# A layer kernel's expert lookup: one-hots from digit codes, fourteen kept tiles, earlier first picks, and a new split of the weighing

## The reference, cut to what matters

```
q = (h @ w_q).reshape(B, S, 8, 2, 128)
s1, s2 = q[..., 0, :] . sub_keys_1, q[..., 1, :] . sub_keys_2     # 128 scores each
v1, i1 = top_k(s1, 16);  v2, i2 = top_k(s2, 16)
cand = v1[:, None] + v2[None, :]                                  # 256 pairs
top, pos = top_k(cand, 16);  eidx = i1 * 128 + i2 at pos          # one of 16384 experts
gate = softmax(top)
act = gelu(einsum('td,tkd->tk', h, expert_u[eidx]))               # 8 * 16 = 128 experts a token
out = einsum('tk,tkd->td', gate * act, expert_v[eidx])            # d = 2048
```

## Time and profile before

| | |
|---|---|
| median of three runs | 1931.37 us |
| the profiled execution, its own time | 1930.16 us |
| its span | 1928.4 us |
| busy PE / DVE / ACT / POOL | 1833.6 / 1317.2 / 389.7 / 750.5 us |
| mean granted clock of PE | 0.985 |

### The profile page before, as it was taken

One profiled execution on the slowest core, in us unless ns is written; L12 is line 12 of the kernel. 1 busy time (PEld: TensorE's weight loads), 2 busy tenths in 40 slices (PEclk: granted clock), 3 DMA queues, 4 the chain that ended last, 5 costly groups with the idle time before them and its releaser, 6 DMA issues.

```text
span 1928.4 us, 28418 instructions
## 1 busy us (share of the span) xinstructions
PE 1833.6 (95%) x10929; PEld 1415.7 (73%) x10929; DVE 1317.2 (68%) x2611; ACT 389.7 (20%) x842; POOL 750.5 (39%) x789
## 2 busy tenths in 40 slices
PE   3899999999999999999999999888989999999997
PEld 3787787777875458888888888778876666656664
DVE  5855666666662333598999975799986666666666
ACT  3022222222222020011111111588740000000001
POOL 2002212222111000365444443338895786744552
PEclk8789999999999999999999999999999999999999
DMA  9956656765581954989999999876449999999997
GB/s 396 420 200 263 228 197 248 292 249 210 213 345 54 402 204 157 370 323 410 405 407 402 402 410 409 327 230 205 144 154 408 409 409 408 409 408 409 409 406 284
DMA packets 124382, 609.09 MB, mean 316 GB/s; under 512 B 15584, under 2 KB 15712, under 8 KB 101216
## 3 DMA queue, kind: packets, MB, share of 16 engines
q1 hardware_dynamic: 66496, 330.33, 44.0%
q0 software_dynamic: 57344, 274.76, 37.3%
q10 hardware_dynamic: 416, 2.25, 0.3%
HBM read 603.09 MB, written 4.19 MB: 315 GB/s over the span
## 4 chain that ended last, share of the span: by engine, by line
PE 81%; DVE 8%; DMA 7%; issue 2%; POOL 2%; ACT 1%; DVEq 0%; SPq 0%; ACTq 0%
PE ps L1413 22%; PE ps L1330 20%; PE ps L996 14%; PE ps L1045 6%; PE ps L1235 6%; DMA arena<-in_v_dense 3%; PE ps L1084 3%; DVE arena L1474 2%; DVE ps L1802 2%; PE ps L1385 2%; DVE arena L1794 2%; DMA arena<-in_ada 2%; POOL arena L615 2%; DMA arena<-in_w_in 1%; PE ps L1356 1%
## 5 line engine op out<-in xcount | busy, mean ns | idle before, releaser
L1413 PE MATMUL ps<-arena 128*128 128x368 f32 x1536 | 477.4, 473 | 7.7 <-DMA arena<-in_v_dense 7.0
L1413 PEld LDWEIGHTS ps<-arena 128*128 128x128 f32 x1536 | 300.9, 196 | 182.8 <-DMA arena<-in_v_dense 10.9
L1863 DVE SCALAR_TENSOR_TENSOR arena<-arena 128x944 f32<-128x944 f32 x254 | 305.2, 1201 | 173.7 <-DMA arena<-in_v_rows,arena 172.3
L599 POOL DMA_INDIRECT arena<-in_u_rows,arena x256 | 257.6, 1006 | 346.6 <-DVE arena L1794 287.2
L1330 PE MATMUL ps<-arena 128*128 128x256 f32 x1792 | 386.9, 379 | 0.0
L1330 PEld LDWEIGHTS ps<-arena 128*128 128x128 f32 x1792 | 340.5, 190 | 46.1
L599 POOL DMA_INDIRECT arena<-in_v_rows,arena x256 | 295.7, 1155 | 182.3 <-DVE arena L1863 149.4
L996 PE MATMUL ps<-arena 128*128 128x256 f32 x1440 | 349.4, 386 | 2.6 <-DMA arena<-in_w_in 2.6
L1794 DVE SCALAR_TENSOR_TENSOR arena<-arena,ps 128x1152 f32<-128x1152 f32 x208 | 277.8, 1349 | 52.8 <-DMA arena<-in_u_rows,arena 52.2
L996 PEld LDWEIGHTS ps<-arena 128*128 128x128 f32 x1440 | 261.8, 190 | 40.6 <-DMA arena<-in_w_in 4.2
L1453 DVE SCALAR_TENSOR_TENSOR arena<-arena 128x2048 f32<-128x2048 f32 x60 | 143.5, 2392 | 24.8 <-DMA arena<-in_ada 24.7
(11 more groups left out here) (251 smaller groups left out, 1746.0 us busy)
## 6 DMA issues: line engine op xcount, KB each, us to landing
arena<-in_ada SPq DMA_DIRECT2D x96, 1024.0 KB, 7.4
arena<-in_v_dense SPq DMA_DIRECT2D x128, 552.0 KB, 8.7
arena<-in_u_dense SPq DMA_DIRECT2D x128, 448.0 KB, 7.1
arena<-in_w_in SPq DMA_DIRECT2D x45, 1024.0 KB, 7.3
arena<-in_w_tail SPq DMA_DIRECT2D x32, 1024.0 KB, 9.1
arena<-in_w_in SPq DMA_DIRECT2D x12, 512.0 KB, 16.6
arena<-in_u_rows,arena POOLq DMA_INDIRECT x256, 10.1
arena<-in_v_rows,arena POOLq DMA_INDIRECT x256, 11.7
```

The source lines that it names most:

```text
L599: nc.gpsimd.indirect_dma_start(out=row, out_offset=None, in_=table[:, :], in_offset=bass.IndirectOffsetOnAxis(ap=i32(idx[:, b, k:k + 1]), ...
L1413: last = mm(sums(b)[:, g, :], dense[:, b, j // 2, :, j % 2], w[:, g * VG:(g + 1) * VG], start=(j == 0), stop=(j == NKEYS - 1))
L1863: stt(total[b], row, w, total[b], ALU.mult, ALU.add).then_inc(v_sum, 1)
```

## The change

It has five parts.

**Codes.** VectorE splits each chosen first key into two digits (`make_digits`) and writes the digits and their squares in bf16; ScalarE's queue stores them to a DRAM tensor `codes` (in the dense u stage, at tile 112). For each group of four tokens a small DMA on SP's queue (`code_tile`, 4 rows of 4x128 bf16) fetches its codes into one of two tiles. One bf16 matmul with prepared weights `code_w` (from 14 more GpSimd instructions ahead of the gathers) leaves a number from which a single Relu with a bias for each partition (`make_bias`) makes the four one-hots. `hot_out` counts one a group instead of two.

**Kept tiles.** Fourteen instead of ten: tiles 18, 24, ... 96. Six of them are loaded during the output projection (`EARLY_KEPT`); `qT` is cut to a quarter for their room.

**First picks.** The transposes of the second keys and `spread_keys(0)` stand before tile 125's products; ScalarE copies and makes the first one-hots before it evacuates tile 126. The exponentials move to tile 112. `turn_weights(0)` stands one group later.

**Dots.** 202 instead of 198 before the picks; in the first half groups 0, 3, ... 27 have none.

**Weighing.** In groups 33, 36, ... 63 VectorE makes all four weights. GpSimd makes five groups' for four u gathers instead of four.

```
@@ loads
+            def keep_tile(n):
+                product_tile(KEPT[KEPT_ORDER.index(n)])
+
             for n in range(6, 22):
...
                 sp.dma_start(ring[:, m % WSLOTS, :], w_tail[n]).then_inc(land[m % WSLOTS], 16)
+                if n in EARLY_KEPT:
+                    keep_tile(EARLY_KEPT[n])
...
+            def code_tile(q):
+
+                b, t = divmod(4 * q, P)
+                if q == 0:
+                    sp.wait_ge(code_zero, 2)
+                    sp.wait_ge(digits_saved, 16 * TB)
+                if q >= 4 and q % 2 == 0:
+                    sp.wait_ge(spread, q - 2)
+                rows = code[q // 2 % 2][4 * (q % 2):4 * (q % 2) + 4, :]
+                sp.dma_start(rows.rearrange("r (t k) -> r t k", t=4), codes[b, t:t + 4].rearrange("t r k -> r t k")).then_inc(code_land[q % 4], 16)
+
+            for q in range(T // 4):
+                code_tile(q)
             for j in range(NKEYS, 2 * NKEYS):
@@ GpSimd
-            for n in range(TB * KTOP):
+            weighed = 0
+            for n in range(NROWS):
...
-                if n >= WEIGH_AT:
-                    weigh(n - WEIGH_AT)
+                while n >= WEIGH_AT and weighed < min(5 * (n - WEIGH_AT + 1) // 4, P // 4):
+                    weigh(weighed)
+                    weighed += 1
@@ ScalarE
+            def one_hot(q):
+
+                act.wait_ge(spread, q + 1)
+                if q >= 2:
+                    act.wait_ge(turned, q - 1)
+                nc.scalar.activation(hot[q % 2].rearrange("p a b -> p (a b)"), bank(0), ACT.Relu, bias=one_minus).then_inc(hot_out, 1)
+
...
                 if j == NKEYS - D // P:
                     act.wait_ge(picked, 8)
+                    act.wait_ge(digits_made, TB)
+                    for b in range(TB):
+                        act.dma_start(codes[b], digits[b]).then_inc(digits_saved, 16)
...
-                nc.scalar.activation(h, bank(0), ACT.Abs, bias=minus_p).then_inc(hot_out, 1)
-                act.wait_ge(hot_out, 2 * q + 1)
-                nc.scalar.activation(h, h, ACT.Relu, bias=ones[:, 0:1], scale=-1.0).then_inc(hot_out, 1)
@@ TensorE
+            def spread_keys(q):
+
+                if q % 2 == 0:
+                    for n in range(2):
+                        pe.wait_ge(code_land[(q + n) % 4], 16 * (q // 4 + 1))
+                if q:
+                    pe.wait_ge(hot_out, q)
+                mm(bank(0), code_w[q % 2], code[q // 2 % 2], start=True, stop=True).then_inc(spread, 1)
+
             for j in range(NKEYS):
+                if j == NKEYS - 3:
...
+                    spread_keys(0)
...
-                if q == P // 4 + 2:
+                if q == P // 4 + 3:
                     turn_weights(0)
@@ VectorE
-                if q >= P // 4 or q % 16 not in (5, 10, 15):
+                if q not in NO_DOT:
                     dots(ndot[0], ndot[0] + 1)
@@ numbers
-LATE = TB * KTOP - 58
-KEPT = tuple(24 + 6 * n for n in range(10))
+LATE = 202
+NO_DOT = (0, 3, 6, 9, 12, 15, 18, 21, 24, 27)
+KEPT = tuple(18 + 6 * n for n in range(14))
+EARLY_KEPT = {8: 2, 10: 3, 12: 4, 14: 5, 16: 12, 18: 13}
...
-WEIGH_AT = TB * KTOP - 24
-POOL_TOKENS = ((2, 3), (3,))
+WEIGH_AT = 232
...
+def pool_tokens(q):
+    return (2, 3) if q < P // 4 else (3,) if q % 3 else ()
```

More of the change, by code:

```diff
@@ L101, in build_layer @@
 def build_layer(nc, x, cols, ada, w_in, w_tail, lora_up, keys,
-                u_dense, u_rows, v_dense, v_rows, out):
+                u_dense, u_rows, v_dense, v_rows, out, codes):
     with ExitStack() as ctx:
@@ L229, in build_layer @@
         top[0] = max(top[0], ring_at + SL)
+        route_at = take(0)
+        repl = new(D // 4)
+        cand = new(2, TOPK * TOPK)
         v16, i16 = new(2 * 2, TOPK), new(2 * 2, TOPK)
         iu = new(2 * 2, TOPK)
-        repl_at = take(0)
-        repl = new(D // 4)
-        cand = new(2, TOPK * TOPK)
-        hot = [view(repl_at, 4, P), view(repl_at + 4 * P, 4, P)]
+        topv, pos, hi_u, lo_u, hi_f, lo_f = (new(2, TOPK) for _ in range(6))
+        hot = [view(route_at + n * 4 * P, 4, P) for n in range(2)]
+        code = [colp[:, 0:2 * P].bitcast(BF16), view(route_at + 8 * P, 2 * P).bitcast(BF16)]
+        assert route_at + 10 * P <= take(0)
         eq = new(2 * TOPK, TOPK)
-        topv, pos, hi_u, lo_u, hi_f, lo_f = (new(2, TOPK) for _ in range(6))
-        iota, minus_p = new(P), new(1)
+        iota, one_minus = new(P), new(1)
         iota16 = iota[:, 0:TOPK]
@@ L242, in build_layer @@
         idx2T = new(T)
-        ident_h = new(P // 2).bitcast(BF16)
-        idx1_h = [new(KTOP // 2).bitcast(BF16) for _ in range(TB)]
         actv, wv = new(TB, KTOP), new(TB, KTOP)
+        digit_at = [take(0) - TB * KTOP, take(2 * KTOP)]
+        digits = [view(a, 2 * KTOP).bitcast(BF16).rearrange("p (t k) -> p t k", t=4) for a in digit_at]
+        code_w = [ones[:, n * KTOP // 2:(n + 1) * KTOP // 2].bitcast(BF16) for n in range(2)]
         assert take(0) <= ring_at + 3 * SL
@@ L604, in _, with number, settled @@
             nc.gpsimd.iota(iota, [[1, P]], base=0, channel_multiplier=0, allow_small_or_imprecise_dtypes=True).then_inc(numbers, 1)
-            nc.gpsimd.iota(minus_p, [[1, 1]], base=0, channel_multiplier=-1, allow_small_or_imprecise_dtypes=True).then_inc(numbers, 1)
+            made = [1]
+            def number(ins):
+                made[0] += 1
+                ins.then_inc(numbers, 1)
+            def settled():
+                pool.wait_ge(numbers, made[0])
+            high, low, coded, part = (view(a, P) for a in (digit_at[0], digit_at[0] + P, digit_at[1], digit_at[1] + P))
+            number(nc.gpsimd.iota(high, [[2, 8], [0, 16]], base=0, channel_multiplier=0, allow_small_or_imprecise_dtypes=True))
+            number(nc.gpsimd.iota(low, [[0, 8], [2, 16]], base=0, channel_multiplier=0, allow_small_or_imprecise_dtypes=True))
+            nc.gpsimd.memset(colp[:, 0:2 * P], 0.0).then_inc(code_zero, 1)
+            for n in range(2):
+                settled()
+                number(nc.gpsimd.affine_select(out=coded, in_=high, compare_op=ALU.is_equal, fill=0.0, base=-4 * n, pattern=[[0, P]], channel_multiplier=1))
+                number(nc.gpsimd.affine_select(out=part, in_=low, compare_op=ALU.is_equal, fill=0.0, base=-4 * n - 2, pattern=[[0, P]], channel_multiplier=1))
+                settled()
+                number(nc.gpsimd.tensor_tensor(coded, coded, part, ALU.add))
+                for r in (1, 3):
+                    settled()
+                    number(nc.gpsimd.affine_select(out=coded, in_=coded, compare_op=ALU.not_equal, fill=-1.0, base=-4 * n - r, pattern=[[0, P]], channel_multiplier=1))
+                settled()
+                number(nc.gpsimd.tensor_copy(code_w[n], coded))
+            assert made[0] == NUMBERS
             pool.wait_ge(w_used, WOUT + 16 + 5)
             def weigh(q):
-                if q % (P // 4) == 0:
+                if not pool_tokens(q):
+                    return
+                if q in (0, P // 4, P // 4 + 1):
                     pool.wait_ge(wT_out, 4 * q // P + 1)
@@ L630, in _ @@
                 if n == 0:
-                    for q in range(TB * KTOP - WEIGH_AT, P // 4):
+                    for q in range(weighed, P // 4):
                         weigh(q)
@@ L1804, in _ @@
             dve.wait_ge(w_used, WOUT + 16 + 2)
[L1805 to L1806 removed]
+            dve.wait_ge(numbers, 1)
             route(0, 0)
@@ L2024 @@
     out = nc.dram_tensor("out_0", (T, D), F32, kind="ExternalOutput").ap()
-    build_layer(nc, *aps, out)
+    codes = nc.dram_tensor("first_key_codes", (TB, P, 4, KTOP), BF16).ap()
+    build_layer(nc, *aps, out, codes)
     r = run(nc, [ins], core_ids=[0])
```

139 lines of the change are left out of this document (85 added, 54 removed).

## The result

The changed kernel took 1939.74 us (median of 6 runs, 1935.48 to 1941.88), the kernel before 1931.3 on the same chip: a ratio of 1.0035, with a 95% interval of 1.0023 to 1.0046. By this ratio it is slower by 6.7 us (4.4 to 8.9; the two medians alone are 8.4 apart), and its median lies outside the range of 1924.5 to 1934.5. Its profiled execution took 1935.48 us, the shortest of the six; the one of before had 1930.16.

The account below looks back on a forecast made before the run. Dense stages were full, so only the 206 us of picking and weighing between them, paced by VectorE, could gain. 1.6 - 5.1 - 0.3 + 3.0 - 1.5 = -2.3 us gave 1929.1 us, range 1924.5 to 1934.5.

Parts of the forecast that it names:

- the split: Weighing behind the last pick: VectorE makes all four weights in every third group, six groups from 6.15 to 5.8 us; -1.5.
- Start of the picks: End of dense u stage: TensorE waits 3.6 us for codes before the first spread, first pick at 1233.7; +1.6 us.
- the upper end: Start of the picks: codes landing after 8.1 us, 2.7, plus 1.7 for a half-speed clock; 4.4 us.
- Rival A: Codes are there in time, no TensorE stop at tile 125, first pick 2.0 earlier; -5.9, 1925.5; chance 0.17.
- Four dots fewer: Picking: 54 instead of 58 dots behind the first pick, 1.28 us of VectorE each; -5.1 us.
- the cheaper one-hots: Picking: a 723 ns ScalarE pass less per group, but ScalarE was idle where VectorE was full; 0.
- rival C: First half of picking: each pair of code tiles comes late, 1.6 x 15 = 24 us slower, 1953; chance 0.08.
- the 2.6 of a short load: Evidence cited against late code tiles in the first half: a 256 KB load alone took 2.6 us.
- The later transpose of the weights: Early picking: `turn_weights(0)` a group later removes a wait of TensorE that reached VectorE; -0.3 us.
- GpSimd's five groups for four gathers: Last four dots: gathers behind more weighing come late, VectorE waiting 1.5 us twice; +3.0 us, bounds 0 and +3.4.
- The v stage: Dense v sums after the weighing: as long as before, 486 to 487 us, moving as a whole.
- D: Early tiles delay the output projection, or the digits delay the dots; up to +6, 1935; chance 0.05.

Follow-up runs that it names:

- e1: Changed kernel with GpSimd weighing one group behind each gather again, not five for four; 1933.34 us, ratio 1.0004 to the kernel before.
- e4: Changed kernel with GpSimd again making one of the four weights in every group of the second half; 1940.94 us, ratio 1.0041 to the kernel before.
- e2: Changed kernel with SP sending the first four code tiles ahead of u tile 122, not behind the last u tile; 1933.74 us, ratio 1.0000.
- e7: Changed kernel with one group of GpSimd's weights behind each gather and the first spread ahead of tile 127, not 125; 1928.24 us, ratio 0.9976.
- e6: Kernel before with one edit alone: five groups of GpSimd's weights behind four gathers; 1936.24 us, ratio 1.0015.
- e9: Changed kernel, codes ahead of u tile 122, GpSimd weighing two groups behind gather 232, one behind every later gather; 1931.40 us, ratio 0.9991.
- e12: Changed kernel unchanged, run again for a second trace; 1937.80 us, ratio 1.0027 to the kernel before.
- e5: Changed kernel, codes ahead of u tile 122, one group of GpSimd's weights per gather, plus TensorE matmuls nobody reads; 1925.59 us, ratio 0.9964.
- e10: e5 with GpSimd again making one weight in every group of the second token block; 1926.22 us, ratio 0.9969 to the kernel before.

## Why the prediction was wrong, step by step

Three steps failed. The wait of TensorE for the codes was mis-sized, and the slow clock behind it stood at nothing in the sum (1.6 forecast, 4.8 measured). GpSimd's lead was priced as late rows alone, and what it does to VectorE's own weights in every group was missed (3.0 forecast, 5.2 measured: 2.7 for the late rows, 2.5 for the collision). And the split was put at -1.5 where it is worth 0.

- **Start of the picks, +1.6: the mechanism was right, the size was not; 4.8.** The codes did queue behind the last u tile. They landed after 7.9 us, not the median 7.0, and left SP a little later against the start of the stage: 1.3 together. The clock fell behind the stall, 1.8, which I had seen in the trace and put only into the upper end, where it belonged in the sum: a dense engine that stands for 4 or 5 us was a surer case than the one-column matmuls from which I took the price. All four traces with the stall have the fall (3.4 us long in two, 6.8 in e1 and e4). The upper end of 4.4 was nearly the value. Run e2 gives the whole term back. Rival A would have needed e2's order, and got 0.9 there, not its 2.0.
- **Four dots fewer, -5.1: right, -4.7.** VectorE had 4.95 us less to do in this half (69.12 and 64.17 busy) and stood 0.2 longer. Nothing came back in the dense stage, whose last dot ended at 1227.6, as forecast. That the cheaper one-hots cost and gain nothing fits this sum; no run has them alone. The codes are in time from group 1 on (no wait of TensorE for them between 1235 and 1298): rival C falls in the changed kernel, but not by much. A pair has 4.4 to 6.3 us from its issue to its spread there, and in e2 and e7 one pair took 5.8 and 5.5 us and held TensorE up for 0.9 and 1.0; the 2.6 of a short load was no price for it. The later transpose of the weights: picks 32 to 36 took 10.0 instead of 10.4, the -0.3, also without a run of its own.
- **GpSimd's five groups for four gathers, +3.0: the wait was right, a second loss was missed.** Picks 60 to 63 took 2.3 us longer, in the second trace 3.4: the late rows, forecast as 3.0, though as one wait of 1.9 to 2.1 and a rest and not as two of 1.5. Missing is the line of VectorE's weights: once GpSimd is as far ahead as its three slots let it be, TensorE's products start its pair, and this puts it onto VectorE's two instructions in every group from the eighth to the twenty-fourth: 0.81 us for 0.60. Picks 48 to 60 lose 1.3, and picks 36 to 48 1.2 (35.6 for 34.4). I had reasoned about GpSimd as a supplier that could only be late, and never asked what it does to VectorE by being early. The trace of the kernel before had it: 0.78 in its groups 24 to 27, and its last dots 2.98 us apart instead of 2.87. e1 takes the lead out of the change, e6 puts it alone into the kernel before, and e9 has the collision without the late rows.
- **The split, -1.5: wrong, 0.** GpSimd has two instructions less in six groups, but they were not what TensorE waited for any more: with slots for three groups, GpSimd can begin a weight only when the products three groups back are done, and the gather then stands between two of them (1414.04, 1415.14 and 1416.19 in the changed kernel). That the gather is what holds the round at 6.2 us is argued from these times; no run moves it. VectorE's instructions for the fourth weight fall beside GpSimd's, which took 0.87 to 0.94 each instead of 0.82. Without a clock fall there are 42.3 us in the changed kernel (e12) and 42.0 before; with TensorE busy 42.6 with and without the split (e5, e10).
- **The v stage**: 487.3 and 488.0 against 486.5 and 487.0. I had it unchanged; other traces of both families lie between 486.5 and 488.0, so no cause is sought.

By the first traces the terms are 4.8 - 4.7 + 4.4 + 0.4 (between the last pick and the last dot) + 1.1 + 0.9 = 6.9 us, where the runs gave 6.7. That they agree so well is partly luck. The two profiled executions themselves are only 5.3 us apart, since the stages ahead of the dense products were 1.8 us shorter in that of the changed kernel (the first dense product comes at 837.7 to 843.2 us in the fourteen traces, in no order that the edits explain). And by the second traces the same terms are 4.3 - 4.9 + 5.5 + 0.0 - 1.9 + 1.0 = 4.0, where the ratio of e12 gives 5.2 (3.1 to 7.4); the weighing behind the last dot is 1.1 in one pair and -1.9 in the other, by where the clock fell. The forecast had -2.3. Of the 9.2 us between it and the first traces 3.2 are the start, 2.6 the split with the clock fall, 2.1 the second half (4.4 and 0.4 where 3.0 less 0.3 stood), 0.9 the v stage and 0.4 the dots. The chances failed too: all rivals but C and D were faster ones, though each price of the slower side (the clock, GpSimd's limit) lay in the rows.

## What to carry to other kernels

A helper engine that runs ahead is not free: when its slots are full, the consumer's pace triggers it at one fixed moment of each round, and if that moment falls on the critical engine's own work of the same kind, every round can pay (here 5%, 0.14 of 2.87 us). When something is moved forward in one engine's program, look at where its data stand in the queue that brings them; two tiles later was as good as a reordered queue. A stall of TensorE in a dense stretch cost the stall and the slow clock behind it in every trace that had one, and matmuls with no purpose in the idle gaps of 2 us behind the last dot were worth 1.7 to 2.4 us of that stretch. Take a second trace before a difference of 2 us is put down to an edit.

## What the runs showed of the hardware that I had not expected

- A 4 KB load on SP's queue behind 448 KB tiles was there 7.9 to 8.1 us after its issue (the changed kernel's two traces), as late as the slowest tile of the earlier trace rows, with the DMA engines full (share 1.01).
- How long VectorE's two weights of 128x128 took went with the moment at which they began in an instruction of GpSimd's. In groups 0 to 27 of the fourteen traces, all 137 pairs begun 0.06 to 0.09 us behind its start took 0.78 to 0.82 us, the 18 at 0.28 to 0.35 us (e5) 0.63 to 0.67, and 165 of the 183 at 0.44 to 0.69 us 0.59 to 0.64. Neither engine stopped for the other. The remaining 18 of the 183 took 0.68 to 0.93, so the offset is not the whole rule, and why the two slow each other no run tells.
- TensorE's granted clock fell to 0.50 for 3.4 us (6.8 in some) at idle stretches of 1.6 to 3.3 us in some executions and not in others of the same program (32 products in 4.12 or 5.4 us, 48 in 5.63 or 7.25).
